# Weight units of the sample stage, asked for by ScalarE on its own DMA queue

## The chip, the core and the metric

The kernel runs on one core of a Trainium2 chip. The core has a matmul engine (TensorE, PE in the views), VectorE (DVE), ScalarE (ACT), GpSimd (POOL) and SyncE (SP), which here does little but issue DMAs. Each engine runs its own instructions in order and meets the others only through semaphores. Transfers between memory (HBM) and the on-chip SBUF are done by 16 DMA engines that all queues share. A queue belongs to the engine that issues into it: q1 is SyncE's, q10 is ScalarE's. The metric is the time of the whole kernel on the device in microseconds (us); lower is better.

## What is computed

One layer of a decoder for a prompt of 512 rows and for 8 samples of 4 new rows each, 1024 positions into their past. A combined projection with `w_in` feeds sparse attention (path A), a pooling mixer (path B) and their gates; a projection with `w_out` and a layer norm end the layer.

```python
h = jnp.einsum('btd,dc->btc', x, w_in)      # q, k, v, gA, q_idx, k_idx, w_idx, u, gB
# A: index scores pick the top 256 keys of each query, which attends to them
s = jnp.einsum('bthd,btkhd->bthk', q, k_sel) * (HEAD_DIM ** -0.5)
o = jnp.einsum('bthk,btkhd->bthd', jax.nn.softmax(where(valid, s, -inf)), v_sel)
# B: trailing means over 2/4/8/16 rows less the row itself, a map per group of 256
mixed = jnp.einsum('btgc,gcd->btgd', mean - u, w_pool) * pool_scale
y = LayerNorm(alpha * x + einsum(concat(o * silu(gA), mixed * silu(gB)), w_out))
```

Keys and values of a sample's past lie in pages of 128 rows (`cache_k`, `cache_v`, 512 KB a page, 8 pages a sample), found through `page_table`. Besides `y` the new keys, values and index keys are put out, and the last 15 rows of `u` (`p_pool`, `s_pool`).

## The kernel before

Everything is in float32. The projections dominate: each 128-column tile of the weights is multiplied with all 544 rows (512 of the prompt, 32 of the samples). To do that at TensorE's faster rate a weight is split in two: ScalarE casts it to a rounded copy (`high`, L675, into `wH`) and GpSimd subtracts that from the original (`low`, L653, into `wL`); TensorE runs three products per tile (L1126). A **unit** is half a weight tile: 128 partitions by 8 x 128 columns, 512 KB. Units live in the four slots of `rawW`, taken in turn. The life of a slot is: the DMA lands (`w_landed`), ScalarE casts (`high_ready`), GpSimd makes the remainder (`stage_ready`), and from then on the slot of `rawW` may be filled again. SyncE's `load_unit` (L437) waits for `stage_ready` of the slot and issues the DMA. The cast of a tile's second half waits besides until TensorE is done with the tile before the last (`tile_ready`), and that of its first half for `stage_free`, as `wH` and `wL` are reused.

The change is in the **sample stage**, some 653 to 948 us of the span. It has four groups, g = 0 to 3, each for two samples and one channel group of the mixer: three turns of one loop (`LOOPS`), then the group that is written out after it (`last`). In a group TensorE works, in an order written out by hand, on

- scores: transposed key pages times the block of queries (L1427). VectorE transposes the pages (L1858, L1859), which arrive in pairs in `kPage`;
- outputs: probabilities times value pages (L1490), which arrive one by one in the four slots of `vPage`, and transposes around them (L1518, L1525, L1532 and others);
- four tiles of weights (eight units), whose results ScalarE copies out (`copy_tile`), and the mixer's own matmuls (L1543).

In a group ScalarE casts units 6 to 13, counted from the group's first, and SyncE asks for units 8 to 15 (`j` in the code): 8 to 11 in the group's first half, 12 to 15 in its second. In groups 0 to 2 these are columns of `u` and gate B of `w_in`; in the last group they are the first of `w_out`.

SyncE's program is `group` from L590 on. For each half of a group it first sends a mask from `dropD`, then for m = 0 to 7: at even m a pair of key pages (`key_unit`, which waits for `k_done` from TensorE), then a unit, and at each m a value page (`value_page`, which waits for `v_free`). All of these transfers go out on q1 in that order.

ScalarE's program in a group is `group` from L1003 on. Its steps for the first half are: `history`, `probs_copied`, `copy_tile(1)`, the cast of unit 6 (`high(TILE_B + 3, 0)`), `last_rows(0)`, the cast of unit 7, `last_rows(1)`, the cast of unit 8, `copy_tile(2)`, the cast of unit 9, `exps` (the softmax's exponentials, L980) and `out_copied("a")` (L689), whose result TensorE takes in L1518. `last_rows(t)` copies rows of `u` from a bank into the small buffer `uN` (L1020, L689) and sends them with two DMAs on q10 (L1024, L1025); before it writes into `uN` it waits on `un_sent` until the two DMAs of the call before have landed:

```python
act.wait_ge(un_sent, 64 * g + 32 * t + 32)
act.activation(uN[0:HIST, 0, :], src[0:HIST, 0:P], ACT.Copy)
...
act.dma_start(p_pool[0, 0, :, col], uN[0:HIST, 0, :]).then_inc(un_sent, 16)
act.dma_start(s_pool[0, :, HIST - NT:HIST, col], uN[:, 1, :]).then_inc(un_sent, 16)
```

Before the change these small writes were all that q10 carried in the stage.

## Time and profile before

| | |
|---|---|
| median of the runs | 1173.95 us (1172.24 to 1175.3, 3 runs) |
| the profiled execution, its own time | 1169.77 us |
| its span | 1168.0 us, mean granted TensorE clock 0.985 |
| TensorE busy | 1126.3 us, 96% of the span |
| VectorE, GpSimd, ScalarE busy | 636.5, 354.4, 318.4 us |
| bytes on q1 and on q10 | 161.40 MB and 8.53 MB |
| time from issue to landing, median | weight unit 3.9 us, key page 5.0, value page 7.0 |

All positions in the program are microseconds from the start of the profiled span. "Granted clock" is TensorE's clock as a share of 2.4 GHz. A wait is put down to the instruction that ended it last; "issue" stands for idle time for which the profile shows nothing that was waited for. In the slices of the span the DMA engines are at least 70% busy in most of the sample stage, and 20 to 40% in the projections ahead of it.

### The profile page before, as it was taken

How to read it: one execution, taken by the hardware profiler on the slowest of the kernel's cores; microseconds unless marked ns; L12 is line 12 of the kernel's file. 1: busy time of each engine (PE TensorE's matmuls, PEld its weight loads, DVE VectorE, ACT ScalarE, POOL GpSimd, SP SyncE). 2: the span in 40 equal slices, each digit the busy share in tenths (PEclk: the TensorE clock that was granted, in tenths of full speed). 3: DMA queues.
4: the chain of work that ended last, by engine and by line, in shares of the span. 5: the costliest groups of instructions: out<-in, count | busy, mean ns of one | idle time of the engine just before them, and what ended most of it. 6: DMA issues, size and time to landing. Idle time of an engine off the chain costs nothing.

```text
span 1168.0 us, 29727 instructions
## 1 busy us (share of the span) xinstructions
PE 1126.3 (96%) x11836; PEld 1048.8 (90%) x11836; DVE 636.5 (54%) x1173; ACT 318.4 (27%) x593; POOL 354.4 (30%) x150
## 2 busy tenths in 40 slices
PE   6999999999999999999997889999999999999995
PEld 5888889999999999999997888888889889999992
DVE  3566667896547557562364574655546443232236
ACT  4333334223332322332231221211212332122111
POOL 2323222333334334333330313221322233443410
PEclk9999999999999999999999999999999999999996
DMA  8542242233333333335414799788878785233103
GB/s 259 135 113 78 64 113 69 80 92 94 83 83 82 83 92 95 88 98 157 118 28 105 245 327 296 259 302 271 302 254 295 231 281 143 73 89 90 54 0 153
DMA packets 202157, 171.56 MB, mean 147 GB/s; under 512 B 22802, under 2 KB 182986, under 8 KB 200818
## 3 DMA queue, kind: packets, MB, share of 16 engines
q1 hardware_dynamic: 188666, 161.40, 44.8%
q10 hardware_dynamic: 13376, 8.53, 2.4%
q8 instruction: 84, 1.38, 0.5%
q14 instruction: 31, 0.25, 0.1%
HBM read 159.57 MB, written 9.90 MB: 145 GB/s over the span
## 4 chain that ended last, share of the span: by engine, by line
PE 82%; DVE 7%; SPq 4%; issue 3%; DMA 3%; ACT 1%; DVEq 0%; ACTq 0%
PE acc L1126 66%; PE acc L1490 2%; PE bank L1184 2%; PE bank L1427 2%; PE acc L1543 2%; PE bank L1301 1%; DVE scoreP L1753 1%; PE bank L1320 1%; DVE top L1749 1%; PE acc L1454 1%; SPq L455 1%; DMA xnat<-in_x_prompt 1%; SPq L561 1%; SPq L458 1%; DVE win L1994 1%
## 5 line engine op out<-in xcount | busy, mean ns | idle before, releaser
L653 POOL TENSOR_TENSOR wL<-rawW,wH 128x1024 fp32r<-128x1024 f32 (+1 forms) x146 | 354.2, 2427 | 766.5 <-ACT wH L675 766.5
L1126 PE MATMUL acc<-actH,wH 128*128 128x272 f32 (+1 forms) x2304 | 493.6, 296 | 1.2 <-DVE actL L1667 1.2
L1126 PE MATMUL acc<-actH,wL 128*128 128x272 f32 (+1 forms) x2304 | 477.6, 289 | 0.0
L1126 PE MATMUL acc<-actL,wH 128*128 128x272 f32 (+1 forms) x2304 | 476.4, 288 | 0.0
L1126 PEld LDWEIGHTS acc<-actH,wH 128*128 128x128 f32 (+1 forms) x2304 | 361.6, 189 | 31.5 <-issue 29.8
L1126 PEld LDWEIGHTS acc<-actL,wH 128*128 128x128 f32 (+1 forms) x2304 | 362.8, 189 | 0.0
L1126 PEld LDWEIGHTS acc<-actH,wL 128*128 128x128 f32 (+1 forms) x2304 | 360.3, 189 | 0.0
L675 ACT ACTIVATE wH<-rawW 128x1024 fp32r<-128x1024 f32 (+1 forms) x146 | 153.2, 1053 | 272.2 <-PE acc L1126 241.2
L2098 DVE SCALAR_TENSOR_TENSOR y<-y,bank 128x512 f32 (+1 forms) x16 | 11.0, 688 | 123.5 <-PE bank L1607 121.5
L1705 DVE SCALAR_TENSOR_TENSOR scoreP<-relu,wiN,scoreP 128x256 f32<-128x256 f32 (+2 forms) x54 | 45.4, 881 | 33.4 <-ACT relu L732 33.4
L1858 DVE STREAM_TRANSPOSE kPage<-kPage 128x1024 f32<-128x1024 f32 x30 | 37.2, 1239 | 46.5 <-DMA kPage<-in_cache_k 45.6
L1915 DVE SCALAR_TENSOR_TENSOR mixed<-bank,gate 128x128 f32<-128x128 f32 x32 | 9.3, 290 | 71.3 <-PE bank L1320 71.3
L732 ACT ACTIVATE relu<-bank 128x512 f32<-128x512 f32 (+3 forms) x63 | 28.9, 502 | 56.4 <-PE bank L1184 33.2
L1427 PE MATMUL bank<-kPage,qBlock 128*32 128x64 f32 x1920 | 34.6, 225 | 8.2 <-DVE kPage L1859 6.1
L1790 DVE MAX8 top<-scoreS 32x8 f32<-32x1056 f32 x32 | 39.9, 1246 | 3.1
L1427 PEld LDWEIGHTS bank<-kPage,qBlock 128*32 128x32 f32 x1920 | 29.9, 113 | 11.8 <-DVE kPage L1859 7.4
L1490 PE MATMUL acc<-vPage,probST 128*4 128x128 f32 x1024 | 38.9, 275 | 1.3 <-issue 0.7
L1793 DVE MATCH_REPLACE8 scoreS<-top,scoreS 32x1056 f32<-32x1056 f32 x32 | 39.4, 1230 | 0.0
L1859 DVE STREAM_TRANSPOSE kPage<-kPage 128x1024 f32<-128x1024 f32 x30 | 36.1, 1202 | 0.0
L1490 PEld LDWEIGHTS acc<-vPage,probST 128*4 128x4 f32 x1024 | 22.9, 87 | 11.5 <-issue 8.6
L1184 PE MATMUL bank<-kiT,raw 64*128 64x256 f32 (+2 forms) x108 | 28.9, 532 | 0.5 <-DVE scoreP L1705 0.5
L2023 DVE SCALAR_TENSOR_TENSOR mixed<-acc,halfscale,raw 128x512 f32 (+3 forms) x16 | 8.0, 502 | 38.9 <-PE acc L1543 38.9
(210 smaller groups left out, 928.3 us busy)
## 6 DMA issues: line engine op xcount, KB each, us to landing
rawW<-in_w_in SPq DMA_DIRECT2D x112, 512.0 KB, 3.9
vPage<-in_cache_v SPq DMA_DIRECT2D x64, 512.0 KB, 7.0
kPage<-in_cache_k SPq DMA_DIRECT2D x60, 512.0 KB, 5.0
rawW<-in_w_out SPq DMA_DIRECT2D x32, 512.0 KB, 3.9
y<-in_x_prompt SPq DMA_DIRECT2D x4, 1024.0 KB, 8.0
out_y_prompt<-y SPq DMA_DIRECT2D x8, 512.0 KB, 2.8
xnat<-in_x_prompt SPq DMA_DIRECT2D x2, 1024.0 KB, 7.7
xnat<-in_x_prompt ACTq DMA_DIRECT2D x2, 1024.0 KB, 11.3
```

The lines of the kernel that those rows point to most:

```text
L653: pool.tensor_tensor(wL[:, slot, :, 0:width], rawW[:, slot, :, 0:width], wH[:, slot, :, 0:width].bitcast(F32), ALU.subtract).then_inc(stag ...
L675: act.activation(wH[:, t.slot, :, 0:width], rawW[:, t.slot, :, 0:width], ACT.Copy).then_inc(high_ready[t.slot], 1)
L732: act.activation(relu[0:rows, t.slot, 0:n], src[0:rows, 0:n], ACT.Relu).then_inc(relu_full[t.slot], 1)
L1126: last = pe.matmul(acc[t.slot][0:width, e, 0:HT], w[:, u.slot, k, 0:width], a[:, kk, e * HT:(e + 1) * HT], start=(half == 0 and k == 0 and ...
L1184: full(b, pe.matmul(take(b)[:, 0:(t + 1) * P], raw[part, slot, t * P:(t + 1) * P], kiT[part, 0:(t + 1) * P], start=True, stop=True))
L1427: last = pe.matmul(bank[b.slot][j * SPAN:(j + 1) * SPAN, at:at + w], qBlock[:, q:q + SPAN], keys[:, :, row:row + STREAK], start=(a == 0 an ...
L1490: return pe.matmul(bank[o.slot][j * SPAN:j * SPAN + NT, a * P:(a + 1) * P], probs, values, start=start and a == 0, stop=stop and a == HALF ...
L1705: dve.scalar_tensor_tensor(sc, relu[:, r.slot, 0:(t + 1) * P], wiN[:, t - 1, ds(h, 1)], sc, ALU.mult, ALU.add).then_inc(bank_free[b.slot], 1)
L1790: own.step(dve.max(top, scores))
L1793: own.step(dve.match_replace(scores, top, scores, PICKED))
L1858: dve.transpose(parts[0], parts[0])
L1859: dve.transpose(parts[1], parts[1]).then_inc(k_turned, 1)
```

## The change

A helper of ScalarE, `load_group_unit`, issues the same DMA for a unit as SyncE's `unit` did: the same bytes, slot, semaphores and wait for `stage_ready`. It is called right behind the cast of unit j - 2 for j = 8 to 15 in each of the four groups, except for units 14 and 15 of the last group, which are asked for at its end, behind `out_copied("b")`. The two calls of `unit` in SyncE's `group` are gone. So 32 transfers of 512 KB go from q1 to q10.

```diff
 # SyncE, group
                     if m % 2 == 0:
                         if m < 4 or not last:
                             key_unit(1 + m // 4, (m // 2 + 2) % UNITS, UNITS + m // 2 + 1, g)
-                        unit(8 + m // 2, last, g)
                     value_page((m + 4) // 8, (m + 4) % 8, g)
...
                             key_unit(2 + m // 4, (m // 2 + 2) % UNITS, 2 * UNITS + m // 2 + 1, g)
-                        unit(12 + m // 2, last, g)
 # ScalarE
+            def load_group_unit(j, last, g):
+                tile, half = j // 2, j % 2
+                t = turn(2 * TILE_B + j, 4, g, 8)
+                act.wait_ge(stage_ready[t.slot], t.free)
+                if last:
+                    view, half, col = wo_view, 1 - half, (tile - 4) * P
+                else:
+                    view, col = w_view, (GB0 if tile % 4 >= 2 else U0) + (2 * (g + tile // 4) + tile % 2) * P
+                stand_alone(act)
+                act.dma_start(rawW[:, t.slot, :, :], view[:, half * HU:(half + 1) * HU, ds(col, P)]).then_inc(w_landed[t.slot], 16)
...
                 high(TILE_B + 3, 0, g, 4)
+                load_group_unit(8, last, g)
                 last_rows(0)
                 high(TILE_B + 3, 1, g, 4)
+                load_group_unit(9, last, g)
                 last_rows(1)
                 high(TILE_B + 4, 0, g, 4)
+                load_group_unit(10, last, g)
                 copy_tile(2, g)
                 high(TILE_B + 4, 1, g, 4)
+                load_group_unit(11, last, g)
                 exps(2 * g + 1)
                 out_copied("a")
                 if last:
                     probs_copied("b")
                     high(TILE_B + 5, 0, g, 4)
+                    load_group_unit(12, last, g)
...
                     high(TILE_B + 5, 1, g, 4)
+                    load_group_unit(13, last, g)
...
                     out_copied("b")
+                    load_group_unit(14, last, g)
+                    load_group_unit(15, last, g)
                     return
...
                 high(TILE_B + 5, 0, g, 4)
+                load_group_unit(12, last, g)
                 high(TILE_B + 5, 1, g, 4)
+                load_group_unit(13, last, g)
                 high(TILE_B + 6, 0, g, 4)
+                load_group_unit(14, last, g)
                 copy_tile(4, g)
                 high(TILE_B + 6, 1, g, 4)
+                load_group_unit(15, last, g)
                 exps(2 * g + 2)
```

In the built program two places show it. The first is ScalarE in the loop of groups 0 to 2, from the cast of unit 6 (L675) to the cast of unit 7. Before, in order, with what each row waits for (L1020 to L1025 are `last_rows(0)`; `hist` is the memory in which `uN` lies):

```order
L675 ACTIVATE wH<-rawW 128x1024 [waits stage_free0,w_landed0]
L417 REGISTER_ALU
L1019 ISA [waits bank_full9]
L1020 ACTIVATE hist<-acc 15x128 [waits un_sent]
L689 ACTIVATE hist<-acc 32x128
L1022 REGISTER_ALU
L1024 ISA [waits bank_free9]
L1024 DMA out_p_pool<-hist 15x128
L1025 ISA
L1025 DMA out_s_pool<-hist 8x4x128
L675 ACTIVATE wH<-rawW 128x1024 [waits tile_ready1,w_landed1]
```

Now (L685 is the cast, L1030 to L1035 are `last_rows(0)`, and L674 is the new helper, here for unit 8):

```order
L685 ACTIVATE wH<-rawW 128x1024 [waits stage_free0,w_landed0]
L674 ISA [waits stage_ready2]
L674 DMA rawW<-in_w_in 128x8x128
L417 REGISTER_ALU
L1029 ISA [waits bank_full9]
L1030 ACTIVATE hist<-acc 15x128 [waits un_sent]
L699 ACTIVATE hist<-acc 32x128
L1032 REGISTER_ALU
L1034 ISA [waits bank_free9]
L1034 DMA out_p_pool<-hist 15x128
L1035 ISA
L1035 DMA out_s_pool<-hist 8x4x128
```

and on ScalarE directly behind these rows, from the cast of unit 7 over the request for unit 9 into `last_rows(1)`:

```order
L685 ACTIVATE wH<-rawW 128x1024 [waits tile_ready1,w_landed1]
L674 ISA [waits stage_ready3]
L674 DMA rawW<-in_w_in 128x8x128
L1029 REGISTER_ALU [waits bank_full9]
L1030 ACTIVATE hist<-acc 15x128 [waits un_sent]
L699 ACTIVATE hist<-acc 32x128
```

The request for unit 8 now stands ahead of the two DMAs of `last_rows(0)` in q10, and the one for unit 9 ahead of the wait on `un_sent` of `last_rows(1)`.

The second place is SyncE in the last group, from its first pair of key pages on. Before (L437 is the unit):

```order
L458 ISA [waits k_done]
L458 DMA kPage<-in_cache_k 128x1024
L458 ISA
L458 DMA kPage<-in_cache_k 128x1024
L437 DMA rawW<-in_w_out 128x8x128 [waits stage_ready2]
L455 TENSOR_LOAD pageT
L455 ISA x2
L458 ISA [waits v_free0]
L458 DMA vPage<-in_cache_v 128x1024
```

Now:

```order
L458 ISA [waits k_done]
L458 DMA kPage<-in_cache_k 128x1024
L458 ISA
L458 DMA kPage<-in_cache_k 128x1024
L455 TENSOR_LOAD pageT
L455 ISA x2
L458 ISA [waits v_free0]
L458 DMA vPage<-in_cache_v 128x1024
```

Between the key pages and the value page the wait for `stage_ready2` and the unit's DMA are gone; nothing else moved.

## Rows read from the trace of the kernel before

**Rows 1.** The page's first part: busy time, share of the span, instructions.

```profile
PE 1126.3 (96%) x11836; PEld 1048.8 (90%) x11836; DVE 636.5 (54%) x1173; ACT 318.4 (27%) x593; POOL 354.4 (30%) x150
```

**Rows 2.** Waits of TensorE, 653 to 948 us: waiting instruction <- releaser: total, times, longest.

```profile
PE bank L1427 <- DVE kPage L1859: 6.1, 3, 2.4
PE acc L1490 <- issue: 2.3, 2, 1.6
...
PE acc L1490 <- DMA vPage<-in_cache_v: 0.6, 1, 0.6
```

**Rows 3.** Waits of SyncE's queue, the same stretch and columns.

```profile
SPq L423 <- POOL wL L653: 3.3, 1, 3.3
```

**Rows 4.** DMA issues of the whole span: count, size of one, median us to landing.

```profile
rawW<-in_w_in SPq DMA_DIRECT2D x112, 512.0 KB, 3.9
...
rawW<-in_w_in SPq DMA_DIRECT2D x2, 320.0 KB, 15.9
```

**Rows 5.** DMA queues from 10.5 to 13 us: packets, MB, share of 16 engines' time.

```profile
q10 hardware_dynamic: 133, 1.00, 94.5%
q1 hardware_dynamic: 134, 0.04, 6.5%
```

**Rows 6.** DMA packets of two stretches, 655 to 658.5 and 712.2 to 713.8 us.

```profile
DMA packets 392, 1.45 MB, mean 414 GB/s; under 512 B 38, under 2 KB 38, under 8 KB 392
...
DMA packets 857, 0.57 MB, mean 357 GB/s; under 512 B 18, under 2 KB 821, under 8 KB 856
```

**Rows 7.** Stretches: us, PE, PEld, DVE, ACT, POOL busy; TensorE clock, DMA share, GB/s.

```profile
804.00:809.00 5.00, 5.00 (x29) 5.00 (x29) 2.22 (x13) 0.51 (x3) 0.00 (x0) 0.66 0.84 232
836.00:845.00 9.00, 8.29 (x184) 7.26 (x183) 7.02 (x21) 2.98 (x6) 2.36 (x1) 1.00 1.05 376
```

**Rows 8.** Timeline of SyncE's queue: start, us, queue, line, transfer, issues.

```profile
743.43 0.87 SPq L458 DMA_DIRECT2D kPage<-in_cache_k  x2
...
820.75 2.02 SPq L458 DMA_DIRECT2D kPage<-in_cache_k  x2
...
896.03 0.86 SPq L458 DMA_DIRECT2D kPage<-in_cache_k  x2
```

**Rows 9.** Timeline of ScalarE, groups 1 and 2; [idle before <- releaser].

```profile
742.42 1.06 ACT L675 ACTIVATE wH<-rawW 128x1024 fp32r<-128x1024 f32 x1 [1.51 <-issue]
...
759.29 1.06 ACT L675 ACTIVATE wH<-rawW 128x1024 fp32r<-128x1024 f32 x1 [0.66 <-DMA rawW<-in_w_in]
...
819.84 1.08 ACT L675 ACTIVATE wH<-rawW 128x1024 fp32r<-128x1024 f32 x1
...
829.65 0.27 ACT L1020 ACTIVATE hist<-acc 15x128 f32<-15x128 f32 x1 [5.69 <-PE acc L1532]
...
839.03 1.06 ACT L675 ACTIVATE wH<-rawW 128x1024 fp32r<-128x1024 f32 x1
...
843.39 0.36 ACT L689 ACTIVATE probST<-acc 128x256 f32<-128x256 f32 x1
```

**Rows 10.** Timeline of GpSimd and of VectorE, group 2.

```profile
840.17 2.36 POOL L653 TENSOR_TENSOR wL<-rawW,wH 128x1024 fp32r<-128x1024 f32 x1 [4.81 <-ACT wH L675]
...
841.01 1.56 DVE L1867 COPY rows<-fewest 128x32 f32<-128x32 f32 x1
```

**Rows 11.** Timeline of TensorE, groups 2 and 3, the output's transposes.

```profile
845.10 0.38 PE L1518 MATMUL acc<-sq,probST 128*128 128x128 f32 x2
...
919.69 0.38 PE L1518 MATMUL acc<-sq,probST 128*128 128x128 f32 x2
```

**Rows 12.** Timeline of ScalarE, group 3.

```profile
905.24 0.27 ACT L1020 ACTIVATE hist<-acc 15x128 f32<-15x128 f32 x1 [5.91 <-PE acc L1532]
...
919.07 0.36 ACT L689 ACTIVATE probST<-acc 128x256 f32<-128x256 f32 x1
...
947.15 0.38 ACT L689 ACTIVATE probST<-acc 128x256 f32<-128x256 f32 x1 [2.76 <-PE acc L1490]
...
959.62 1.06 ACT L675 ACTIVATE wH<-rawW 128x1024 fp32r<-128x1024 f32 x1 [4.49 <-PE acc L1126]
```

## The prediction

> **What bounds the kernel now.** I read the page first. TensorE is busy 96% of the span, every other engine 54% or less [rows 1]. So the change can pay only where TensorE stands still in the sample stage, and can cost only where it makes TensorE stand still anew. The waits of TensorE between 653 and 948 us are short [rows 2]: 6.1 us in three stalls for transposed keys (at 664.6, 682.6 and 759.6), 0.6 us for a value page (761.9), 2.3 us in which nothing that the profile shows is waited for, and small ones. The first key stall comes before anything that the change touches. What could be won is therefore 2.4 + 1.6 + 0.6 = 4.6 us of waiting, plus some clock.
>
> **Is SyncE really held up by weight units?** Between 653 and 948 it waited for GpSimd's remainder (`stage_ready`) once, 3.3 us, ahead of the very last unit of the stage (unit 15 of the last group) [rows 3], behind which no page is queued. So the change doesn't free SyncE from a wait; it takes 32 issues of about 0.4 us each off its queue and moves 16 MB to another queue.
>
> **Part 1, the bytes leave q1.** A weight unit is 1024 packets of 512 B; a key or value page is 128 packets of 4096 B. In a stretch of pages alone, 392 packets (354 of them large) took all 16 engines for 3.5 us: 3.5 x 16 / 354 = 0.158 us a packet, so 8 packets an engine, 1.27 us a page. In a stretch of mostly weights 1.6 us x 16 went into 35 large and 803 packets of 512 B: (25.6 - 5.5) / 803 = 0.025 us, 64 an engine, 1.6 us a unit [rows 6]. Pages asked for behind a unit come that much sooner.
> What I expect for the three places: the stall at 682.6 stays mostly, as VectorE and not the page is late there (no wait for a DMA is among the causes); 0.5 us off. In group 1 both the page of keys and the value page are late by their bytes, and each has one or two units ahead of it in q1: 1.6 + 0.6, of which I take 1.8. Sum: 2.3 us won, between 0 and 4.6.
>
> **Part 2, how two queues share.** This is the step on which the sign rests. At the kernel's start both queues are full: SyncE's holds rows of 320 B, ScalarE's rows of 8192 B. Between 10.5 and 13 us q10 moved 133 packets and q1 134, with 94.5% and 6.5% of the engines' time [rows 5]. The engines take one packet of each in turn, whatever its size. That is why this first pair of units (320 KB) took 15.9 us to land where 512 KB takes 3.9 us later on [rows 4]. So while pages are waiting in q1, a unit in q10 gets one packet for each page packet: 64 x (0.158 + 0.025) = 11.7 us where it took 1.6 us. Pages lose little, 0.025 on 0.158.
> The Trainium skill, "DMA: Bandwidth & Descriptors", section "Queues, rings and completion order", says that an engine goes round its queues by packets, a packet being some 9 to 17 descriptors. The trace agrees as far as it can: 133 against 134. By the rule as by the row a unit's share is 512 : 4096 in bytes, and the sum is the same.
>
> **Part 3, what is queued on ScalarE.** 32 issues at about 0.4 us are hidden: each stands where ScalarE waits 1.5 to 9 us for TensorE next. Two come later than before, units 14 and 15 of the last group: asked for behind the output's copy, at 947.5, while the casts of the last units queued there stand at 959.6 and later; 12 us for a transfer of 3.9 [rows 4, 12], so nothing.
> The price is behind the new DMAs. In each group ScalarE now runs: cast of unit 6, ask for unit 8, `last_rows(0)` with its two small writes, cast 7, ask for 9, `last_rows(1)`, cast 8, ask for 10, `copy_tile(2)`, cast 9, ask for 11, `exps`, `out_copied`. `last_rows(1)` waits (`un_sent`) until the writes of `last_rows(0)` have landed, and these now lie in q10 behind unit 8. Everything after it waits for that, and the cast of unit 9 for unit 9's own bytes.
> How much room is there? In group 2 ScalarE goes cast 9 at 839.03 [rows 9]; GpSimd's remainder follows at 840.17 for 2.36 us; VectorE's COPY of the softmax, begun at 841.01, ends as GpSimd ends (842.57) [rows 10]; the output is copied at 843.39 to 843.75 [rows 9], and TensorE takes it at 845.10 [rows 11]. So room is 1.35 us. In group 3 the same chain has 0.3 us or less: the copy ends at 919.43 [rows 12] and TensorE takes it at 919.69 [rows 11].
> Now the groups in turn. The time from issue to first packet is 3.9 - 1.6 = about 2.2 us (an estimate from rows 4 and 6).
> Group 0: unit 8 goes out before the pages of 666.6 and is in early; 0.
> Group 1: unit 9 is asked for at 743.5, unit 8 one cast earlier, the pages only at 743.4 [rows 8, 9]. Unit 8 is through before; unit 9 takes 745.7 + 11.7 = 757.4, plus up to 2 us since engines don't end together, and its cast was at 759.3. 0 as well.
> Group 2: SyncE asks for pages at 820.75 [rows 8], ScalarE for unit 8 at 820.9. Unit 8 is in at 823.1 + 11.7 = 834.8 if the backlog is unbroken; `last_rows(1)`, at 829.65 before [rows 9], goes at 835.5 to 836.5, its two issues and cast 8 take 2.9 us, and `copy_tile(2)` (1 us ahead of cast 9 before) starts at 839 to 840. Unit 9 then has from 835 on: 836.5 to 838 if q1 runs empty for 2 us, 847 if it doesn't. The engines were 105% busy from 836 to 845 [rows 7], but with units in it, which now leave 5 us of gaps. So cast 9 is late by between 1 and 8 us, and after the 1.35 us of room TensorE stands for 0 to 6.6 us. I take 3.0, a little under the middle, for the gaps.
> Group 3: the same start (pages at 896.0 [rows 8], unit 8 within a microsecond of it), in at 910.5; `last_rows(1)`, at 905.24 before [rows 12], goes at 911.5, `copy_tile(2)` about 1 us late, and there is no room. Unit 9 has a thinner q1 by then (no keys for a next pair). Between 1.2 and 8 us; I take 2.5, near the lower end.
> Clock: of the four stalls over 1.5 us in the stage two were followed by a stretch at half clock (granted 0.66 over 804 to 809, so 3.4 us at 1.2 GHz) [rows 7], in which 3.4 us of matmuls cost 1.7 more. Two new such stalls for one that goes: +0.7.
>
> **The sum**: -0.5 - 1.8 + 3.0 + 2.5 + 0.7 = +3.9 us. On the profiled execution, 1169.8 (span 1168.0), that gives 1173.7; the median of the runs is 1173.95, 4.2 above it, and the prediction is 1173.95 + 3.9 = 1177.8.
>
> **Rivals.**
> *Wash.* Pages are asked for as TensorE frees slots, so q1 often runs empty, a unit needs just 1.6 us of that, and casts stay in time: only the group 3 delay of 1 us against 1 to 2 us won: 1173.5, at most +-3. For it: 4 pages are 5.1 us of each 9 us round. Against it: the share of 105%.
> The Trainium skill, same page, section "Issuing engines are not separate DMA queues", holds that a second issuing engine saves no more than the sequencer's issue time. Here issue time is not what TensorE waits for, so by that rule nothing changes: 1173.95, inside this rival. The trace agrees in so far as the engines are the same and full.
> *Gain.* If units fit into gaps and pages come sooner everywhere, all 4.6 us and one stretch of half clock (1.7) go, less 1 for group 3: 1173.95 - 5.3 = 1168.7. Against it: the stall at 682.6 is VectorE's, and those marked "issue" have nothing to do with it.
> *Starved.* The slowest of the 16 engines lags by 2 us in a full stretch, the delay of each group moves the next one's requests together, and `copy_tile(2)` becomes late too (TensorE has a single accumulator in this stage and can't start unit 12's tile before it): 3 us in groups 0 and 1, 6.6 and 4 in 2 and 3, three drops of clock: -0.5 + 3 + 3 + 6.6 + 4 + 5 - 5 of overlap = +16, 1190. It decides from the point where unit 9 lands later than 1.4 us after its cast of before.
>
> **Chances.** The forecast (late casts in groups 2 and 3) 0.38; starved 0.17; wash 0.30; gain 0.15. About 0.3%, 3.5 us, is what a measurement of this kernel can tell from no change. Of the forecast's +1 to +9 two thirds lie beyond it: slower 0.25 + 0.17 + a little of the wash = 0.45; faster 0.17, same 0.38. The range of 8 in 10 cuts most of the gain's far end and of the starved case's: 1169.5 to 1189; the forecast's own is 1175 to 1183.
>
> **What the new profile would show.** Right: q10 with 16.8 MB more; units taking 6 to 12 us to land instead of 3.9; a wait of ScalarE in `last_rows(1)` and before the cast of unit 9 for a DMA; TensorE idle before the L1518 transposes of groups 2 and 3 (before: none) and the key stall at 759.6 gone. Wrong: casts at the same distance from TensorE's work as before, or units in q10 landing in 4 to 5 us while pages are in flight: then the packets don't alternate as at the start, and the forecast falls to the wash or the gain.

## Result: faster, where slower was forecast

The changed kernel takes 1166.07 us (median of 10 runs, 1163.83 to 1169.89), the kernel before 1172.47 us in the same comparison (10 runs, 1167.22 to 1175.62): ratio 0.9947, 95% interval 0.9928 to 0.9966, 6.2 us faster. The forecast was 1177.8, with a range of 1169.5 to 1189.0; the time lies below it, near the rival "gain" (1168.7, to which I gave 0.15).

Both kernels were run once more in the study:

> The changed kernel once more, unchanged, beside the padded one. From the first ten runs 0.9947; from two kernels that keep its loop and its queues 0.9963. Expected 0.995 to 0.996, stretches of the 2nd to 4th group again 35.5, 39.9, 35.4, 39.1, 35.4 us within 0.5.

> The kernel before once more, unchanged, for a second profile of it: ratio 1.000 +- 0.002. The key stalls near 664, 682 and 759 and the value page's at 761 should be there again if they belong to the kernel; the stalls marked issue at 803.65 (1.6 us) and 840.46 (0.7) should be elsewhere or missing if they are chance, and at the same places if they are the kernel's.

The changed kernel came to 0.9954 (0.9939 to 0.9970), the kernel before to 1.0004 (0.9992 to 1.0017). The second profile of the latter has key stalls at 668, 678, 686 and 765 and a stop marked issue at 807.0 to 808.5, at the same matmul as the one at 803.65 before: these belong to the kernel. The stop of 0.7 us at 840.46 is there again with 0.3 us.

The profiled execution of the changed kernel has a span of 1164.3 us. The lines are 10 to 22 higher in the new file: L675 is L685 now, L1427 is L1449, L1490 is L1512, L1518 is L1540, L1126 is L1148; the new DMA is L674. First the engines, the queues and the DMA issues of units, from the page of the kernel after:

```profile
PE 1127.7 (97%) x11836; PEld 1051.0 (90%) x11836; DVE 639.1 (55%) x1173; ACT 318.2 (27%) x593; POOL 354.0 (30%) x150
...
q1 hardware_dynamic: 155386, 144.62, 39.2%
q10 hardware_dynamic: 46656, 25.31, 7.7%
...
rawW<-in_w_in ACTq DMA_DIRECT2D x24, 512.0 KB, 8.4
...
rawW<-in_w_out ACTq DMA_DIRECT2D x8, 512.0 KB, 4.7
```

The bytes have moved as announced (q10 from 8.53 to 25.31 MB), and a unit on q10 takes 8.4 us to land where one on q1 took 3.9 [rows 4]. That much of the prediction held. Now the waits of TensorE between 653 and 948 us, columns as in [rows 2]:

```profile
PE bank L1449 <- DVE kPage L1881: 3.4, 2, 2.2
PE bank L1499 <- issue: 1.0, 1, 1.0
PE acc L1540 <- issue: 0.9, 1, 0.9
...
PE acc L1512 <- issue: 0.4, 1, 0.4
```

Against [rows 2] one key stall of three is gone (6.1 us to 3.4; those left are in group 0), the value page's 0.6 us is gone, and "issue" ahead of L1490 fell from 2.3 us to 0.4. No wait of TensorE for a late cast has come in their place.

Where did the time go? TensorE's timeline has a mark in every half group: the 64 small matmuls L1477 (after: L1499). Kernel before, then after:

```profile
731.48 0.76 PE L1477 MATMUL bank<-sq,probS 128*32 128x32 f32 x64
...
769.39 0.76 PE L1477 MATMUL bank<-sq,probS 128*32 128x32 f32 x64
```

```profile
734.19 0.76 PE L1499 MATMUL bank<-sq,probS 128*32 128x32 f32 x64
...
769.69 0.76 PE L1499 MATMUL bank<-sq,probS 128*32 128x32 f32 x64
```

From mark to mark that is 37.9 us before and 35.5 after. Each profile has its own zero, and the stage starts some us sooner or later in it, so times of two profiles are compared as distances from such a mark. Read so for all profiles taken in this study (an undisturbed first half of a group takes 35.3 us, an undisturbed second half 39.1 or, in group 1, 39.7), the stretches that differ are:

| kernel | group 0, 1st half | group 1, 1st | group 1, 2nd | group 2, 1st | timed ratio |
|---|---|---|---|---|---|
| before, e0_before | 42.5, 44.5 | 37.9, 37.0 | 42.6, 42.5 | 36.4, 35.9 | 1 |
| after, e12_after | 41.9, 41.8 | 35.5, 36.1 | 39.9, 40.6 | 35.4, 35.4 | 0.9947, 0.9954 |
| e1_time_back | 42.0 | 36.4 | 39.6 | 37.1 | 0.9984 |
| e2_before_no_bytes | 40.5 | 36.4 | 39.6 | 35.8 | 0.9961 |
| e3_after_no_bytes | 40.3 | 35.4 | 39.7 | 35.4 | 0.9939 |
| e4_first_half | 42.8 | 39.2 | 40.8 | 37.6 | 1.0010 |
| e5_second_half | 43.0 | 38.4 | 40.0 | 36.4 | 0.9981 |
| e7_unit14 | 43.0 | 37.2 | 39.8 | 37.0 | 1.0003 |
| e8_padded, e15_padded | 41.7, 42.9 | 36.4, 36.6 | 43.0, 40.2 | 35.4, 36.0 | 0.9974, 0.9958 |
| e9_before_unrolled | 42.7 | 35.4 | 41.1 | 35.4 | 0.9992 |
| e10_after_unrolled | 42.6 | 36.0 | 40.1 | 35.5 | 0.9965 |
| e6_late_ask | 44.0 | 35.4 | 39.9 | 36.4 | 1.0060 |
| e11_keys_first | 41.6 | 35.9 | 39.6 | 35.7 | 0.9962 |
| e13_units67 | 40.5 | 35.3 | 39.8 | 35.3 | 0.9942 |
| e14_units67_keys | 39.1 | 35.4 | 40.0 | 35.5 | 0.9906 |

Mean of two profiles before less mean of two after: 1.7, 1.7, 2.3 and 0.8, together 6.4 us, about what the timing gives. So the gain lies in four places: group 0's first half, the stalls for pages in the first halves of groups 1 and 2, and the second half of group 1.

Part of it is clock. In the stage TensorE has stretches of 3.4 us at a granted clock of 0.50 (1.2 GHz), and each costs 1.7 us. The two profiles before have two and three of them (664.8 and 804.7; 6.8 us from 687.2 on, and 810.1), the two after one each (678.7 and 678.2), and full clock elsewhere. That is 2.6 of the 6.4 us, 0.9 in group 0 and 1.7 in group 1's second half. Group 0's share is thus the least certain: its two values before differ by 2 us through such a stretch, and e10, with the same queues as the changed kernel, has 42.6 there.

### The profile page after: what moved, and what is told of

Read it like the earlier page. It is cut to its first block, busy times and chain, and to the rows that moved or that the text cites. A ratio compares the mean times of both kernels' runs of the same rounds, so it can differ in the third digit from the quotient of the medians.

```text
span 1164.3 us, 29726 instructions
## 1 busy us (share of the span) xinstructions
PE 1127.7 (97%) x11836; PEld 1051.0 (90%) x11836; DVE 639.1 (55%) x1173; ACT 318.2 (27%) x593; POOL 354.0 (30%) x150
## 3 DMA queue, kind: packets, MB, share of 16 engines
q1 hardware_dynamic: 155386, 144.62, 39.2%
q10 hardware_dynamic: 46656, 25.31, 7.7%
## 4 chain that ended last, share of the span: by engine, by line
PE 86%; DVE 6%; SPq 3%; DMA 2%; issue 2%; ACT 1%; DVEq 0%; ACTq 0%
PE acc L1148 69%; PE acc L1512 3%; PE bank L1449 2%; PE bank L1206 2%; PE acc L1565 2%; PE bank L1323 1%; DVE scoreP L1775 1%; PE bank L1342 1%; DVE top L1771 1%; PE acc L1476 1%; DMA xnat<-in_x_prompt 1%; SPq L561 1%; PE bank L1258 1%; DVE y L2185 1%; DMA kPage<-in_cache_k 1%
## 5 line engine op out<-in xcount | busy, mean ns | idle before, releaser
L1148 PE MATMUL acc<-actH,wH 128*128 128x272 f32 (+1 forms) x2304 | 494.1, 296 | 1.0 <-DVE actL L1689 1.0
L1148 PE MATMUL acc<-actH,wL 128*128 128x272 f32 (+1 forms) x2304 | 478.2, 289 | 0.0
L1148 PE MATMUL acc<-actL,wH 128*128 128x272 f32 (+1 forms) x2304 | 477.1, 289 | 0.0
L1148 PEld LDWEIGHTS acc<-actH,wH 128*128 128x128 f32 (+1 forms) x2304 | 362.0, 189 | 31.4 <-issue 29.8
L1148 PEld LDWEIGHTS acc<-actL,wH 128*128 128x128 f32 (+1 forms) x2304 | 363.2, 189 | 0.0
L1148 PEld LDWEIGHTS acc<-actH,wL 128*128 128x128 f32 (+1 forms) x2304 | 360.9, 189 | 0.0
L685 ACT ACTIVATE wH<-rawW 128x1024 fp32r<-128x1024 f32 (+1 forms) x146 | 153.1, 1053 | 268.7 <-PE acc L1148 236.7
L1880 DVE STREAM_TRANSPOSE kPage<-kPage 128x1024 f32<-128x1024 f32 x30 | 37.2, 1239 | 45.5 <-DMA kPage<-in_cache_k 44.6
L1812 DVE MAX8 top<-scoreS 32x8 f32<-32x1056 f32 x32 | 39.9, 1247 | 3.1
L1449 PE MATMUL bank<-kPage,qBlock 128*32 128x64 f32 x1920 | 34.5, 224 | 5.2 <-DVE kPage L1881 3.4
L1512 PE MATMUL acc<-vPage,probST 128*4 128x128 f32 x1024 | 39.0, 275 | 0.0
L1449 PEld LDWEIGHTS bank<-kPage,qBlock 128*32 128x32 f32 x1920 | 29.9, 112 | 8.3 <-DVE kPage L1881 4.1
L1881 DVE STREAM_TRANSPOSE kPage<-kPage 128x1024 f32<-128x1024 f32 x30 | 36.1, 1202 | 0.0
L1512 PEld LDWEIGHTS acc<-vPage,probST 128*4 128x4 f32 x1024 | 23.1, 87 | 10.1 <-issue 7.8
L2016 DVE SCALAR_TENSOR_TENSOR win<-win,wtab 128x676 f32<-128x676 f32 (+2 forms) x24 | 28.4, 1181 | 1.7 <-DVE win L2016 0.9
```

The costliest lines, as they stand in the source:

```text
L685: act.activation(wH[:, t.slot, :, 0:width], rawW[:, t.slot, :, 0:width], ACT.Copy).then_inc(high_ready[t.slot], 1)
L1148: last = pe.matmul(acc[t.slot][0:width, e, 0:HT], w[:, u.slot, k, 0:width], a[:, kk, e * HT:(e + 1) * HT], start=(half == 0 and k == 0 and ...
L1449: last = pe.matmul(bank[b.slot][j * SPAN:(j + 1) * SPAN, at:at + w], qBlock[:, q:q + SPAN], keys[:, :, row:row + STREAK], start=(a == 0 an ...
L1512: return pe.matmul(bank[o.slot][j * SPAN:j * SPAN + NT, a * P:(a + 1) * P], probs, values, start=start and a == 0, stop=stop and a == HALF ...
L1812: own.step(dve.max(top, scores))
L1880: dve.transpose(parts[0], parts[0])
```

## Why units landing late cost nothing

The prediction's dearest terms, +3.0 and +2.5, are zero. ScalarE's timeline of the kernel after in group 2, with its DMA issues (ACTq):

```profile
817.14 0.38 ACTq L674 DMA_DIRECT2D rawW<-in_w_in  x1
...
817.42 1.08 ACT L685 ACTIVATE wH<-rawW 128x1024 fp32r<-128x1024 f32 x1
...
820.53 1.06 ACT L685 ACTIVATE wH<-rawW 128x1024 fp32r<-128x1024 f32 x1 [1.52 <-issue]
820.86 0.39 ACTq L674 DMA_DIRECT2D rawW<-in_w_in  x1
827.23 0.27 ACT L1030 ACTIVATE hist<-acc 15x128 f32<-15x128 f32 x1 [5.64 <-PE acc L1554]
...
836.62 1.06 ACT L685 ACTIVATE wH<-rawW 128x1024 fp32r<-128x1024 f32 x1
```

and the two issues of units in it, from narrow windows of the DMA view (unit 8, then unit 9; the last column is us to landing):

```profile
rawW<-in_w_in ACTq DMA_DIRECT2D x1, 512.0 KB, 5.2
```

```profile
rawW<-in_w_in ACTq DMA_DIRECT2D x1, 512.0 KB, 14.0
```

SyncE asks for its key pages at 817.92. Unit 8 goes out at 817.14, so it lands in 5.2 us, not 11.7; unit 9 meets the pages and takes 14.0 us, landing at 834.9, and its cast stands at 836.62. So 2.2 + 11.7 us was the time of a unit, but of the wrong one. Two steps failed. I took the request to leave when the cast ends (820.9 in the profile before). ScalarE's sequencer issues it sooner, here 0.28 us before the cast even starts (unit 9: 0.33 us after the start of its cast), and that puts unit 8 0.8 us ahead of the pages instead of just behind them. And I then let unit 9 start behind unit 8's landing at 835, where in group 1 I had let it start at once: 13.9 to 15.9 us from asking to landing by that sum, 13.9 measured (745.53 to 759.41). The wait on `un_sent` that I feared behind unit 8 came once, 2.1 us.

That the sum fits is in part luck. One packet of each queue in turn fits the trace where q1 is full: from 678 to 687 us, with unit 10 of group 0 in q10 (17.7 us to landing), q1 moved 870 packets and q10 830. In the middle of unit 9's 14 us, from 824 to 828, it was otherwise:

```profile
q1 hardware_dynamic: 296, 1.08, 68.2%
q10 hardware_dynamic: 853, 0.43, 36.5%
```

There q1 left gaps, as the rival "wash" had it, and q10 took them. Thirteen of the 16 engines had finished unit 9 by 830.8; the last one ended at 834.9, and that one sets the landing.

The prediction also took no account of casts that were late before the change. ScalarE's waits for units in the stage, kernel before:

```profile
ACT wH L675 <- DMA rawW<-in_w_in: 11.7, 5, 5.8
```

Of these 5.8 us are for unit 6, which the change doesn't touch; the other four, 5.8 us together, are for units 8 and 9 of groups 0 and 1 (one is in [rows 9], 0.66 at 759.29). After, only unit 6's is left (5.6 us, the first of the rows below). SyncE asked for unit 8 of group 1 at 744.70, 13.2 us behind the mark, and it landed 7.1 us later; ScalarE asks 7.6 us behind its mark and has it in 5.1.

How near was the edge? Unit 9 lands 1.8, 1.7 and 1.4 us ahead of its cast in groups 1 to 3. One kernel asks for each unit one cast later:

```diff
                 high(TILE_B + 3, 0, g, 4)
-                load_group_unit(8, last, g)
                 last_rows(0)
                 high(TILE_B + 3, 1, g, 4)
-                load_group_unit(9, last, g)
+                load_group_unit(8, last, g)
                 last_rows(1)
                 high(TILE_B + 4, 0, g, 4)
-                load_group_unit(10, last, g)
+                load_group_unit(9, last, g)
```

> The changed kernel, but each unit is asked for one cast later: unit j behind the cast of unit j - 1 (14 and 15 together behind the cast of 13). It asks what the late landings on q10 would cost if the room were gone. In the changed kernel unit 9 lands 13.9, 14.0 and 14.9 us after it is asked for and 1.8, 1.7 and 1.4 us ahead of its cast. Asked for one cast later, units 8 and 9 land some 3 to 8 us after ScalarE is free for their casts, copy_tile(2) and the copy of the attention output behind them are late, and TensorE waits for them: 2 to 6 us in each of three or four groups, ratio 1.000 to 1.012. If instead the landings follow the asking at 4 to 6 us or the casts have room elsewhere, it stays at 0.995.

It took 1175.87 us, ratio 1.0060 (1.0032 to 1.0088): about 12 us slower than the changed kernel. ScalarE's waits for units, kernel after and e6_late_ask, 653 to 948 us, and one of TensorE's in e6_late_ask:

```profile
ACT wH L685 <- DMA rawW<-in_w_in: 5.6, 1, 5.6
```

```profile
ACT wH L685 <- DMA rawW<-in_w_in: 60.8, 13, 7.9
...
ACT wH L685 <- DMA rawW<-in_w_out: 7.6, 2, 6.2
```

```profile
PE acc L1541 <- issue: 1.9, 2, 1.0
```

So late units do cost time, as the rival "starved" has it, and the room for unit 9 is some 1.5 us. How the 12 us come about isn't seen. Of the two stops of TensorE ahead of the output's transposes (L1541 here) only the 0.8 us in group 2 are where the prediction put them; the other, 1.0 us in group 0, is in the kernel after too (0.9). The profiled execution was the fastest of its ten (1168.1 of up to 1183.7), and its stretches are longer in group 0 (44.0) and group 2 (36.4) only.

## What the gain is made of

**Requests for pages.** The prediction asked whether SyncE waits for weight units and, as it did so only once [rows 3], took its queue for free. That was the wrong question. These are SyncE's waits for TensorE, 660 to 930 us, kernel before and after (each is time in which it could ask for a page as soon as the slot is free):

```profile
SPq L458 <- PE bank L1427: 19.5, 11, 2.6
SPq L458 <- PE acc L1490: 13.5, 8, 2.9
SPq L423 <- PE bank L1480: 7.5, 4, 2.3
```

```profile
SPq L458 <- PE acc L1512: 42.3, 17, 12.6
SPq L458 <- PE bank L1449: 30.3, 17, 2.6
SPq L423 <- PE bank L1502: 18.7, 6, 5.3
```

40.5 us against 91.3. Before, SyncE was mostly behind: it found the slot free and was late itself. A unit costs it about 0.8 us (the wait's instruction, registers, the issue), and its issues of pages and units between 655 and 925 us took 13.6 us more than 0.4 each; after, 3.8, and 6.1 in e2_before_no_bytes below, where the units' bytes are gone from q1. One more of its costs went by itself, the jump back to the start of its loop. SyncE's timeline around it, before and after (last value page of group 0, first mask of group 1):

```profile
731.50 0.33 SPq L458 DMA_DIRECT2D vPage<-in_cache_v  x1
737.97 1.71 SPq L514 DMA_DIRECT2D probS<-dropD  x2
```

```profile
733.23 0.33 SPq L458 DMA_DIRECT2D vPage<-in_cache_v  x1
735.45 0.79 SPq L514 DMA_DIRECT2D probS<-dropD  x1
```

The branch itself ends at 732.00, and the next instruction starts at 737.58; after, 0.26 us lie between. Its body is 329 instructions long before and 294 after. In the profiles of this study the jump takes 0.3 us for 294 instructions, every time, and 4.2 to 6.1 us for 312 to 330. The Trainium skill, "Runtime: NRT & Kernel Launch", section "Instruction fetch mechanics", says that a taken branch to code outside the two blocks at hand has to fetch it first; that fits, though by its sizes (two blocks of 256 instructions) 329 could have fitted too. The measurement decides.

What the jump does to the pages is seen in the first pair of keys behind it, here after and in e9_before_unrolled (below), a kernel that keeps all units with SyncE on q1 but has no jump:

```profile
742.56 0.86 SPq L458 DMA_DIRECT2D kPage<-in_cache_k  x2
```

```profile
742.42 0.87 SPq L458 DMA_DIRECT2D kPage<-in_cache_k  x2
```

The marks stand at 734.19 and 734.04, so both ask 8.4 us behind it; before it was 743.43 [rows 8] against 731.48, 12.0 us. For groups 1 and 2 of each kernel:

| kernel | instructions in the loop | jumps, us | first keys behind the mark, us |
|---|---|---|---|
| before | 329 | 5.6, 5.0 | 12.0, 8.7 |
| e0_before | 329 | 5.7, 5.6 | 11.6, 9.6 |
| after, e12_after | 294 | 0.3, 0.3 | 8.4, 8.4 |
| e9_before_unrolled, e10_after_unrolled | no loop | none | 8.4, 8.4 |
| e1_time_back | 318 | 4.8, 4.3 | 10.8, 10.3 |
| e2_before_no_bytes | 325 | 5.1, 4.2 | 10.9, 10.2 |
| e4_first_half | 312 | 6.1, 5.6 | 12.4, 11.4 |
| e8_padded | 330 | 4.7, 5.0 | 10.7, 8.4 |
| e15_padded | 330 | 5.5, 5.0 | 11.0, 9.9 |

(In e8 TensorE itself reached group 2's mark 3 us late, through its longest stop marked issue, 1.95 us, and slow clock; so its keys aren't late against the mark there, and the half group takes 35.4.)

In the second halves of the groups, with no jump ahead of them, the first keys are asked for 8.2 to 8.3 us behind the mark in every kernel, before as after. So SyncE's lateness at the start of groups 1 and 2 comes from the jump, not from the 0.8 us of each unit. In e9 SyncE issues every unit and asks for the four pairs of group 1's first half at 8.4, 14.2, 22.6 and 28.5 us, the changed kernel at 8.4, 13.9, 22.6 and 28.7, the kernel before at 12.0, 18.3, 24.2 and 32.3. In these two places it was the 35 instructions fewer in the loop that let SyncE ask sooner.

Further kernels ask what time and bytes are worth. e1_time_back leaves the units on ScalarE and puts SyncE's time back (this also brings the body to 318 instructions and the jump to 4.8 us):

```diff
                         if m < 4 or not last:
                             key_unit(1 + m // 4, (m // 2 + 2) % UNITS, UNITS + m // 2 + 1, g)
+                        page_number(ck, 0)
```

> The changed kernel, but where SyncE used to issue a weight unit in `group` it now looks up a page number and drops it: no transfer, no wait for another engine, only about 0.8 us of SyncE's own time, as the issue of a unit took (key page at 743.96 + 0.34 to value page 746.11 before is 1.81 us, 743.08 + 0.33 to 744.42 in the changed kernel is 1.01). The bytes stay on ScalarE's queue. Theory SyncE's time (the gain of 6.2 us comes from pages that are asked for sooner): most of the gain goes, ratio to the kernel before 0.998 to 1.001, SyncE's waits for TensorE between 660 and 930 fall from 91 us back towards 60, a key stall comes back. Theory bytes (it comes from units no longer lying ahead of pages in q1): ratio stays 0.993 to 0.996.

0.9984 (0.9973 to 0.9996): two thirds of the gain are gone though all bytes are still on q10. Its waits for TensorE are back at 62 us. As it brings back issue time and jump together, it doesn't part the two. The next kernels take the bytes away instead, on SyncE's and on ScalarE's queue. Both load only 8 KB for each of the 24 units of groups 0 to 2 and compute with what the slots held before, so their output isn't the layer's:

```diff
+                elif tile >= 4:
+                    sp.wait_ge(stage_ready[t.slot], t.free)
+                    stand_alone(sp)
+                    sp.dma_start(rawW[0:16, t.slot, 0:1, 0:P],
...
```

> The kernel before, with the 24 unit transfers of groups 0 to 2 cut from 512 KB to 8 KB (16 rows of 512 B), still issued by SyncE in their old places (the weights of those units are stale, so the output is not the reference's). SyncE keeps its issue time and its waits, q1 loses the bytes. Theory SyncE's time: at most a small gain, ratio 0.997 to 1.000, from the 14 us that SyncE spends in issues longer than usual. Theory bytes: the whole gain of the change or more, ratio 0.990 to 0.995.

> The changed kernel with the same cut of the 24 unit transfers of groups 0 to 2 to 8 KB, on ScalarE's queue (stale weights again). SyncE has neither the issues nor the bytes beside it. If the units' bytes still cost something in the changed kernel, this is faster than the changed kernel's 0.9947: 0.990 to 0.993 by the theory bytes; 0.994 to 0.995 by SyncE's time, since TensorE then waits only where VectorE is late.

0.9961 (0.9947 to 0.9975), between the two theories, and 0.9939 (0.9924 to 0.9953), not apart from the changed kernel. So bytes count as well as time: without the bytes, but with SyncE's time and its jump, most of the gain is there, and without both nothing more is to be had. e1 has q1 free of the bytes too and gained less; the two differ in that its units still land through q10, and their intervals just overlap. In the changed kernel, where SyncE is in time, the units' bytes on q10 cost TensorE nothing that could be measured.

e8_padded (run again as e15) makes the changed kernel's loop as long as before with instructions that SyncE runs where it waits anyway:

```diff
                 if not last:
+                    for _ in range(36):
+                        stand_alone(sp)
                     mask(2, "Ptb", g)
```

> The changed kernel, with 36 one-instruction increments of an unused semaphore put into the body of SyncE's loop, ahead of the second mask, where SyncE waits 4.6 us for TensorE anyway (766.3 to 770.9). They cost some 0.06 us each, hidden there, but make the loop's body 330 instructions long instead of 294, as long as before (329). In the profiles so far the jump back to the loop's start takes 0.3 us with 294 instructions (three kernels) and 4.3 to 6.1 us with 312 to 329 (six). Theory jump (much of the gain comes from SyncE's loop no longer having to fetch its code again): the jump takes 4 to 6 us again, the mask and the key pages behind it are late, stalls of TensorE for keys in group 1 and 2 come back, ratio 0.997 to 0.999 as with the time put back. Theory issue time (0.8 us for each unit on SyncE): the padding costs nothing, ratio 0.9945 +- 0.0015 as the changed kernel.

> The changed kernel with 36 padding instructions in SyncE's loop again, for the difference to e12 in the same call. Theory jump: 2 to 3 us slower than e12 (0.9975), with the stretch that holds 803 at 42 to 43 us or the first half of group 1 at 36.4 and more. Theory issue time: no difference to e12.

0.9974 (0.9961 to 0.9987) and, beside a second timing of the changed kernel (0.9954), 0.9958 (0.9942 to 0.9973). The jump was back both times (4.7 to 5.5 us), the keys of group 1 went out 2.3 and 2.6 us later, and its first half took 36.4 and 36.6 us, as expected of the jump; by the timings it cost between nothing and 3 us. The kernel before without the jump:

```diff
-            with sp.Fori(0, LOOPS) as g:
+            for g in range(LOOPS):
                 group(g, False)
```

> The kernel before, with SyncE's loop over the groups written out three times (units still with SyncE, on q1): no jump back, and fewer register instructions. Theory jump: SyncE loses the two stops of 5.6 us, key and value stalls of groups 1 and 2 shrink, ratio 0.996 to 0.998; the stall for code at 803.65 stays, since the units' bytes are still in q1. Theory issue time: SyncE still issues each unit, ratio 0.999 to 1.001.

0.9992 (0.9978 to 1.0007), where 0.996 to 0.998 was expected if the jump counts, though the first halves of groups 1 and 2 are undisturbed in its profile (35.4), 2.1 and 0.8 us shorter than the means before. The same on the changed kernel:

> The changed kernel with SyncE's loop written out as well. Its jump takes 0.3 us already, so by the theory jump nothing is left to win there: ratio 0.993 to 0.9955, the stretches of the 2nd to 4th group within 0.3 us of the changed kernel's 35.5, 39.9, 35.4, 39.1, 35.4 us. If it is slower than that, straight code has a fetch cost of its own.

0.9965 (0.9953 to 0.9978), no gain on the changed kernel, and rather a loss (0.993 to 0.9955 was expected). So profiles and timings part here: in the profiles the jump alone sets how late the pages of groups 1 and 2 are asked for, and the stretches follow; in the timings taking it away is worth 1 us, with an interval of up to 2.6. Whether the written-out program costs something elsewhere, as e10 hints, isn't shown, and the jump's share of the 6.2 us stays open.

**The stall marked "issue".** The prediction set it aside ("those marked issue have nothing to do with it"). TensorE's timeline before and after, at the same matmuls:

```profile
801.43 0.61 PE L1490 MATMUL acc<-vS,probSTn 32*4 32x128 f32 x14
803.65 0.38 PE L1490 MATMUL acc<-vS,probSTn 32*4 32x128 f32 x2 [1.62 <-issue]
```

```profile
801.74 0.61 PE L1512 MATMUL acc<-vS,probSTn 32*4 32x128 f32 x14
802.72 0.38 PE L1512 MATMUL acc<-vS,probSTn 32*4 32x128 f32 x2 [0.38 <-issue]
```

The stop stands behind the same matmul in all 18 profiles, before the last two of L1490 in that half, and a 16 KB packet on q8, the queue that the profile calls "instruction", always starts 2.2 to 2.7 us before it ends. That TensorE waits there for its next code is inferred from this. Two windows of 0.1 us of the DMA view, before at 800.9 and after at 800.4:

```profile
q1 hardware_dynamic: 64, 0.03, 110.2%
q8 instruction: 1, 0.02, 71.9%
```

```profile
q8 instruction: 1, 0.02, 57.6%
```

Before, the code's packet starts 1.1 us ahead of the last matmul that was at hand; after, 1.9 us. So the stop is longer the later the packet starts, and not through the time from its start on. Then comes slow clock (0.66 [rows 7], that is 3.4 us at 1.2 GHz) before and none after. Of the five stops of 1.3 us or more here, those of before, e0 and e8 were followed by such a stretch, those of e4 (1.3) and e9 (1.6) were not. What lies in q1 there before is unit 14, asked for at 796.8 between the key and the value pages. One kernel moves only this unit of each group:

```diff
                         if not last:
                             key_unit(2 + m // 4, (m // 2 + 2) % UNITS, 2 * UNITS + m // 2 + 1, g)
-                        unit(12 + m // 2, last, g)
+                        if m != 4:
+                            unit(12 + m // 2, last, g)
```

> The kernel before, with a single unit of each group, unit 14, asked for by ScalarE (behind the cast of unit 12); all others stay with SyncE. Before, unit 14 of group 1 was issued at 796.8, landed 801.7 to 803.5, and TensorE stood still for code at 802.04 to 803.65. If these bytes ahead of a fetch of code are what makes the 42.6 us stretch, it falls to 39.9 to 40.5 with this one unit gone, and the ratio is 0.997 to 0.998. If it is SyncE's lateness as a whole, the stretch stays above 42.

The stretch fell from 42.6 to 39.8 us and the stall to 0.3, as expected. In the four profiles with unit 14 and its bytes on q1 (before, e0, e4, e9) the stall is 1.3 to 1.6 us; in the fourteen others it is 0.1 to 1.1, but once 1.95 (e8). So it is mostly, not only, that unit. But the timed ratio was 1.0003 (0.9983 to 1.0023) where 0.997 to 0.998 was expected: the timing doesn't confirm what the one profiled execution shows, and how much of the gain this unit carries stays open.

The halves of the groups, one with SyncE and the other with ScalarE:

> Only units 8 to 11 of each group are asked for by ScalarE, 12 to 15 stay with SyncE. By the traces so far the gain has two sources: pages asked for sooner in the first half of groups 1 and 2 (the stalls at 759.6, 761.9 and 840.5: 2.0 + 0.8 us) and, in the second half of group 1, one stall of TensorE marked issue at 803.65 with the drop of its clock behind it (2.7 us: the stretch from one score transpose to the next is 42.6 and 42.5 us in two profiles of the kernel before, 39.9 without the units' bytes on q1 or without their issue). Here the first goes and the second stays: stretches 35.5, 42.5, 35.4 us for the 2nd group's halves and the 3rd group's first, ratio 0.997 to 0.998. A single cause (SyncE's time over the whole group) would give half of the 0.9947, 0.9973, with the 42.6 at 41 or less.

> The counterpart: only units 12 to 15 are asked for by ScalarE, 8 to 11 stay with SyncE. Two sources: the key and value stalls of the first halves stay (stretches 37 to 38 and about 36 us), the 42.6 us stretch falls to 39.9; ratio 0.997 to 0.998.

1.0010 (0.9992 to 1.0027) and 0.9981 (0.9962 to 1.0001). The second is as expected. The first is a miss: even the half group that was to gain got worse, 39.2 us instead of 35.5.

```profile
PE bank L1442 <- DVE kPage L1874: 9.4, 6, 2.4
```

Each of the two leaves SyncE with 312 instructions in its loop and so with the jump, which by the table above keeps SyncE late; so the parts don't add up (0.9991 for both together, 0.9947 measured). In e4 the jumps take 6.1 and 5.6 us and the first keys of group 1 go out 12.4 us behind the mark, 0.4 later than before. The first of them then takes 4.8 us to land, where it took 3.6 before. There are six key stalls, 9.4 us. The one in group 1 takes 1.9 us (1.6 before) and is followed by 3.4 us at a granted clock of 0.50, which the kernel before doesn't have there; with the stall and 1.7 us for that clock all but 0.3 us of the 39.2 are accounted for.

## What is left, and a faster kernel

After the change the key stalls left are in group 0. There SyncE still issues units 6 and 7 into a full queue. SyncE's timeline of the kernel after:

```profile
656.05 0.85 SPq L458 DMA_DIRECT2D kPage<-in_cache_k  x2
657.02 2.83 SPq L437 DMA_DIRECT2D rawW<-in_w_in  x2
660.30 6.75 SPq L514 DMA_DIRECT2D probS<-dropD  x4
669.18 0.90 SPq L458 DMA_DIRECT2D kPage<-in_cache_k  x2
```

The four masks take 6.75 us, and the next keys go out at 669.18. The first try asks for the second key pair sooner:

```diff
+            key_unit(1, 1, UNITS)
             value_page(0, 1)
             value_page(0, 2)
             value_page(0, 3)
-            key_unit(1, 1, UNITS)
```

> The changed kernel with the second pair of key pages of the prologue asked for ahead of value pages 1 to 3 instead of behind them. Group 0 still has two key stalls, at 667.1 and 677.9 (1.3 and 2.2 us, with slow clock behind them): the pair asked for at 656.0 lands at 664.6 and is transposed until 667. Asked for 3.5 us sooner it lands by 661 to 662 and the first stall goes, unless value page 1 is then late; the second moves with SyncE's next requests. If key stalls are set by the time of asking, ratio 0.991 to 0.994; if by VectorE alone, 0.9945.

0.9962 (0.9939 to 0.9985): the first stall went, the second grew from 2.2 to 3.5 us, and the half group stayed at 41.6, where 0.991 to 0.994 was expected. The second try gives units 6 and 7 to ScalarE too; the third does both:

```diff
             high(TILE_B + 2, 0)
+            load_group_unit(6, False, None)
             high(TILE_B + 2, 1)
+            load_group_unit(7, False, None)
```

> The changed kernel, with units 6 and 7 of the prologue asked for by ScalarE too, behind the casts of units 4 and 5 (647 and 648 us) instead of by SyncE at 657. There SyncE's issue of unit 7 takes 2.3 us and the first of the four masks 4.2, since q1 is full, and the next pair of key pages goes out at 669.2. If the key stalls of group 0 (667.1 and 677.9, 3.4 us and 3 us of slow clock) come from SyncE being late, that pair goes out 2 to 6 us sooner, the second stall goes, and the first half of group 0 takes 37 to 39 us instead of 41.9: ratio 0.990 to 0.993. If VectorE sets them, nothing changes: 0.995.

> The same, with the second pair of key pages of the prologue ahead of value pages 1 to 3 as in e11, where the first stall went and the second grew from 2.2 to 3.5 us. With SyncE free sooner both should be gone: first half of group 0 at 36 to 38 us, ratio 0.989 to 0.992; if VectorE or PE's requests set them, as e13.

e13 came to 0.9942 (0.9925 to 0.9958), e14 to 0.9906 (0.9885 to 0.9927) with 1161.38 us (4 runs), 10.5 us faster (medians) than the kernel before and faster than the changed one (0.9954, timed beside it) beyond both intervals. e13 isn't apart from the changed one and misses its expectation (0.990 to 0.993). Group 0's first half takes 40.5 and 39.1 us instead of 41.8. SyncE's timeline of e13_units67, and TensorE's waits of e14_units67_keys:

```profile
656.60 0.85 SPq L458 DMA_DIRECT2D kPage<-in_cache_k  x2
657.91 3.34 SPq L514 DMA_DIRECT2D probS<-dropD  x4
663.61 0.86 SPq L458 DMA_DIRECT2D kPage<-in_cache_k  x2
```

```profile
PE bank L1450 <- DVE kPage L1882: 1.9, 1, 1.9
PE acc L1566 <- DVE mixed L2046: 0.7, 2, 0.4
PE acc L1513 <- issue: 0.5, 1, 0.5
```

The keys go out 5.6 us sooner (10.0 us behind the mark instead of 16.0). But in e13 that didn't shorten the waits: it has three key stalls, 4.1 us, against 3.4 and 3.9 us in the two profiles of the kernel after, and is shorter only because the 3.4 us at half clock are missing in its group 0. Only with the reordered keys one stall is left (1.9 us), with half clock behind it; so e14's gain needs both, and e13 alone doesn't show that SyncE's lateness sets these stalls.

The prediction blamed VectorE for one of them ("the stall at 682.6 stays mostly, as VectorE and not the page is late there"). VectorE's timeline of the kernel before:

```profile
680.17 1.25 DVE L1858 STREAM_TRANSPOSE kPage<-kPage 128x1024 f32<-128x1024 f32 x1
```

The pair had been asked for at 673.08 and 673.60 and was there at 679.74, 6.1 us after the second request, so VectorE began 0.4 us behind the landing. It transposes a pair in two steps of 1.2 us; the releaser in the row is only the last link.

## The prediction, step by step

- *What bounds the kernel.* Right: only the stage's stalls could move. The list of what could be won (4.6 us) was too short: it left out the stop marked issue with its slow clock (2.3 us in the mean of the profiles) and group 0 (1.7 us, half of it clock).
- *SyncE is not held up.* Wrong, and it made the gain too small. I read its waits for GpSimd, took its own time at nothing, and had not looked at the jump: in the profiles the first keys of group 1 were asked for 12.0 us behind the mark, in the changed kernel 8.4.
- *Part 1.* The places were right (group 1's key and value stalls gone: 1.7 us over the first half of group 1, 1.8 forecast), so the size is luck in part: the reason was bytes ahead of the pages. Key pages on q1 did not land sooner after their request (median 5.9 us after, 5.0 before); they were asked for sooner. The row for 682.6 was forecast to stay; it went, while one at 677.9 came.
- *Part 2.* Right where q1 is full, and units did become slow: 8.4 us in the median, up to 17.7. But q1 wasn't full all the time, and pages paid more than "little": the median key page takes 0.9 us longer.
- *Part 3.* Wrong, the step that cost the sign: 5.5 us for late casts in groups 2 and 3, 0 measured, through the time of the request (unit 8 of group 2 landed in 5.2 us, not 13.9) and the unit that takes the load. The 0.7 us for clock hung on it; measured were 2.6 us the other way. Without both the sum would have been -2.3, with the stop marked issue about -4.6.
- *The rule of the Trainium skill* ("DMA: Bandwidth & Descriptors", section "Issuing engines are not separate DMA queues": only the sequencer's issue time is saved, usually small) gave no change. Measured is 0.9947. What this case shows beside it is that issues moved away also shorten the loop (329 to 294 instructions) and change the order of the bytes.
- *Chances.* 0.17 for faster was too little for a kernel whose page requests were visibly late; the rival "gain" came out in size, but the reason given against it (the stalls marked issue "have nothing to do with it") was wrong.

## To carry to other kernels

Before a queue is called free, look at how often its engine waits for the consumer whose slots it fills: a requester that seldom waits may be the late one, whatever its other waits say. Look for gaps in its own program too, such as the jump at the end of a loop. A stall is put down to its last link; follow it back to the time of the request. Compare requests as distances from a mark in the consumer's work. And a transfer that has long been given room may share a queue poorly and still cost nothing, so work out landing against need for each, from the instant the sequencer issues and not from the end of the instruction ahead.

## What the runs showed of the hardware

- A jump back over 294 instructions of SyncE takes 0.3 us, over 312 to 330 it takes 4.2 to 6.1 us.
- TensorE stops at a fixed matmul for 0.1 to 1.95 us, and a 16 KB packet on its instruction queue starts 2.2 to 2.7 us before the stop's end in all 18 profiles. It shows as "issue".
- With both queues busy a 512 KB unit in rows of 512 B took 10 to 18 us beside pages in rows of 4096 B, and 3.9 to 5.2 us when asked for just before them.
- Of the 16 engines' parts of one such unit thirteen were in by 830.8 us and the last at 834.9.
- ScalarE's sequencer issued a DMA 0.28 us before the start of the cast that stands ahead of it in the program.
